# Experts' weights four rows at a time: fewer, larger loads into fewer, larger slots

## What is computed

```python
def expert_choice_moe(h, router_w, w_gate, w_up, w_down):
    affinity = jax.nn.softmax((h @ router_w).astype(F32), axis=-1)
    gate, idx = lax.top_k(jnp.swapaxes(affinity, 1, 2), cap)
    xe = jax.vmap(lambda hb, ib: hb[ib])(h, idx)
    hid = jax.nn.silu(jnp.einsum('becd,edf->becf', xe, w_gate)) * jnp.einsum('becd,edf->becf', xe, w_up)
    ye = jnp.einsum('becf,efd->becd', hid, w_down) * gate[..., None].astype(h.dtype)
```

## Time and profile before

| | |
|---|---|
| median of three runs | 3330.03 us (3327.26 to 3331.25) |
| the profiled execution | 3335.36 us |
| its span, first to last instruction | 3333.6 us |
| TensorE (PE) busy in the span | 3009.6 us, 90% |
| DMA moved | 431.71 MB in 130595 packets |
| first gate product of the experts | at 2690.03 us |
| end of the last w_down product | at 3322.50 us |

### The profile page before, as it was taken

One profiled execution on the slowest core, in us unless ns is written; L12 is line 12 of the kernel. 1 busy time (PEld: TensorE's weight loads), 2 busy tenths in 40 slices (PEclk: granted clock), 3 DMA queues, 4 the chain that ended last, 5 costly groups with the idle time before them and its releaser, 6 DMA issues. The chain is left out here.

```text
span 3333.6 us, 44206 instructions
## 1 busy us (share of the span) xinstructions
PE 3009.6 (90%) x18941; PEld 1781.4 (53%) x18941; DVE 1235.9 (37%) x2363; ACT 650.1 (20%) x1446; POOL 250.5 (8%) x347
## 2 busy tenths in 40 slices
PE   5999998999899899979999978899999789999998
PEld 2344664446675555558888863366444444444443
DVE  1052451384442499415555546544001411111111
ACT  2111341111332454112112111433100100000000
POOL 0000110000010000004324310110000000000000
PEclk8999999998879899989999989999999899999999
DMA  6441013230002311000000012300521269999998
GB/s 230 151 151 51 1 51 95 88 76 27 1 1 74 140 51 51 12 28 3 2 2 3 2 44 98 126 1 1 209 76 51 87 274 427 427 427 427 427 427 362
DMA packets 130595, 431.71 MB, mean 130 GB/s; under 512 B 28978, under 2 KB 40502, under 8 KB 102621
## 3 DMA queue, kind: packets, MB, share of 16 engines
q1 hardware_dynamic: 130402, 428.89, 33.3%
HBM read 418.21 MB, written 10.66 MB: 129 GB/s over the span
## 5 line engine op out<-in xcount | busy, mean ns | idle before, releaser
L333 PE MATMUL banks<-weight_ring,rows_turned 128*128 128x512 f32 (+1 forms) x1576 | 683.1, 594 | 52.2 <-DMA weight_ring<-in_w_in 30.5
L333 PEld LDWEIGHTS banks<-weight_ring,rows_turned 128*128 128x128 f32 x1576 | 301.2, 197 | 426.7 <-issue 406.8
L2402 PE MATMUL banks<-rows_turned,weight_ring 128*128 128x256 f32 (+1 forms) x768 | 252.8, 489 | 1.6 <-PEq L1364 1.3
L2402 PEld LDWEIGHTS banks<-rows_turned,weight_ring 128*128 128x128 f32 x768 | 147.2, 192 | 100.5 <-issue 85.7
L3615 PE MATMUL banks<-weight_ring,chosen_turned 128*64 128x512 f32 (+1 forms) x696 | 174.3, 558 | 9.5 <-DMA weight_ring<-in_w_up 6.5
L3615 PE MATMUL banks<-expert_weights_early,chosen_turned 128*64 128x512 f32 (+1 forms) x672 | 169.3, 558 | 11.2 <-DMA expert_weights_early<-in_w_up 7.6
L1432 PE MATMUL banks<-weight_ring,mix_turned 128*128 128x512 f32 x320 | 138.8, 594 | 3.8 <-ACT mix_turned L1445 2.0
L3717 DVE TENSOR_TENSOR hidden<-hidden,banks 128x512 f32<-128x512 f32 (+1 forms) x24 | 14.0, 639 | 324.2 <-PE banks L3615 324.2
L2637 PE MATMUL banks<-v_channels 64*64 64x64 f32 (+1 forms) x2880 | 122.7, 233 | 1.0 <-ACT v_channels L2757 0.3
L2637 PE MATMUL banks<-weight_ring 64*64 64x64 f32 (+1 forms) x2880 | 116.5, 227 | 0.5
L333 PE MATMUL banks<-weight_ring,branch_turned 128*128 128x512 f32 x256 | 112.8, 594 | 1.9 <-PE banks L333 1.1
(11 more groups left out here) (551 smaller groups left out, 4417.3 us busy)
## 6 DMA issues: line engine op xcount, KB each, us to landing
weight_ring<-in_w_gate SPq DMA_DIRECT2D x29, 1408.0 KB, 17.2
weight_ring<-in_w_up SPq DMA_DIRECT2D x29, 1408.0 KB, 15.1
expert_weights_early<-in_w_gate SPq DMA_DIRECT2D x28, 1408.0 KB, 19.0
expert_weights_early<-in_w_up SPq DMA_DIRECT2D x28, 1408.0 KB, 15.7
expert_weights_early<-in_w_down SPq DMA_DIRECT2D x36, 1024.0 KB, 17.3
weight_ring<-in_w_down SPq DMA_DIRECT2D x35, 1024.0 KB, 17.5
weight_ring<-in_l_w_in SPq DMA_DIRECT2D x15, 2048.0 KB, 8.6
weight_ring<-in_w_in SPq DMA_DIRECT2D x13, 2048.0 KB, 7.8
```

The costliest lines, as they stand in the source:

```text
L333: ins = kit.nc.tensor.matmul(self.bank(u), lhsT, rhs, start=(k == 0), stop=(k == nk - 1))
L2402: ins = nc.tensor.matmul(kit.ps[:, bank(u), 0:n], w[:, k, f * P:(f + 1) * P], hT[:, k, h0:h0 + n], start=(k == 0), stop=(k == KD - 1))
```

## The change

A slot holds four rows per partition, 4 x 1408 elements, 22 KB, and there are five: two early, two in the ring, one late. A chunk has 512 rows (the last of down 384: three per partition), so a partition's run is 22 KB for gate and up, 16 KB and 12 KB for down. A pair of experts has 14 chunks instead of 28. Contracted indices go in fours where they went in pairs. The tile of the weighted choice gives way to the larger late slot and lies in what the ring has left over (`spare`). The file grows by one line, so that L3615 before is L3616 after.

```diff
-    ROOM = 2 * 1408
+    ROOM = 4 * 1408
...
-        self.rooms += [flat[:, i * self.ROOM:(i + 1) * self.ROOM] for i in range(4)]
+        self.rooms += [flat[:, i * self.ROOM:(i + 1) * self.ROOM] for i in range(2)]
         self.slots = 0
+        self.spare = flat[:, 2 * self.ROOM:2 * self.ROOM + 2 * SEQ]
...
-                for k0 in range(0, KD, 2):
+                for k0 in range(0, KD, 4):
                     for e in (2 * p, 2 * p + 1):
-                        self.plan.append((2, FF, a[name][0, e][k0 * P:(k0 + 2) * P, :]))
-            for f0 in range(0, NF, 2):
-                n = min(2, NF - f0)
+                        self.plan.append((4, FF, a[name][0, e][k0 * P:(k0 + 4) * P, :]))
+            for f0 in range(0, NF, 4):
+                n = min(4, NF - f0)
...
-            at = slice(f * P, (f + 1) * P) if c < 24 else slice(f // 2 * 2 * P + f % 2, (f // 2 + 1) * 2 * P, 2)
+            at = slice(f * P, (f + 1) * P) if c < 24 else slice(f, 512, 4)
...
-                sp.dma_start(ada_b[:, 24:40].rearrange("p (i j) -> p i j", j=2), as_pairs(a["ada_b_2"][0, 3 * D:5 * D])).then_inc(c_landed.sem, 16)
+                sp.dma_start(ada_b[:, 24:40].rearrange("p (i j) -> p i j", j=4), as_fours(a["ada_b_2"][0, 3 * D:5 * D])).then_inc(c_landed.sem, 16)
...
-        early = sb("expert_weights_early", [P, 4, ExpertStream.ROOM])
+        early = sb("expert_weights_early", [P, 2, ExpertStream.ROOM])
...
-                nc.vector.tensor_scalar(normed[:, t, :].rearrange("p (i j q) -> p i q j", j=2, q=P), x[:, t, :].rearrange("p (i q j) -> p i q j", j=2, q=P),
+                nc.vector.tensor_scalar(normed[:, t, :].rearrange("p (i j q) -> p i q j", j=4, q=P), x[:, t, :].rearrange("p (i q j) -> p i q j", j=4, q=P),
...
-        weighted = sb("choice_weighted", [P, 2, TX, P])
+        weighted = weights.spare.rearrange("p (i t n) -> p i t n", i=2, t=TX)
...
-                    for k0 in range(0, KD, 2):
-                        c = W * p + 8 * mat + k0
+                    for k0 in range(0, KD, 4):
+                        c = W * p + 4 * mat + k0 // 2
...
-                        src = hid[:, f // 2 * 2 * P + f % 2:(f // 2 + 1) * 2 * P:2] if f < NF - 1 else hid[:, f * P:]
+                        src = hid[:, f0 * P + f - f0:f1 * P:f1 - f0]
...
-                for f0 in range(0, NF, 2):
-                    n = min(2, NF - f0)
-                    c = W * p + 16 + f0
+                for f0 in range(0, NF, 4):
+                    n = min(4, NF - f0)
+                    c = W * p + 8 + f0 // 2
...
-                act.wait_ge(weights.used, W * p + 8)
+                act.wait_ge(weights.used, W * p + 4)
```

More of the change, by code:

```diff
@@ L1296, in row_bc, with as_fours @@
     return v.partition_broadcast(n)
-def as_pairs(v):
-    return v.rearrange("(i p j) -> p i j", p=P, j=2)
+def as_fours(v):
+    return v.rearrange("(i p j) -> p i j", p=P, j=4)
 def as_columns(v):
@@ L2851, in second_half @@
         g2 = sb("norm2_gain", [P, KD])
-        load(kit, [(const[:, :], a["constants3"]), (g2[:, :].rearrange("p (i j) -> p i j", j=2), as_pairs(a["norm2_g_2"][0]))])
+        load(kit, [(const[:, :], a["constants3"]), (g2[:, :].rearrange("p (i j) -> p i j", j=4), as_fours(a["norm2_g_2"][0]))])
         latent_attention(kit, stream, m, a, x, s_park, h_park, y_park)
@@ L2943, in sync @@
                 sp.dma_start(normed[:, :, :], y_park).then_inc(delta_landed.sem, 16)
-                sp.dma_start(router[:, :, :].rearrange("p (i j) e -> p i j e", j=2), a["router_w_2"][0].rearrange("(i p j) e -> p i j e", p=P, j=2)).then_inc(loaded.sem, 16)
+                sp.dma_start(router[:, :, :].rearrange("p (i j) e -> p i j e", j=4), a["router_w_2"][0].rearrange("(i p j) e -> p i j e", p=P, j=4)).then_inc(loaded.sem, 16)
                 sp.dma_start(rows[:, :, :].rearrange("p i n -> p (i n)"), row_bc(rows_park[0])).then_inc(loaded.sem, 16)
@@ L3607, in gate_and_up @@
                         pe.wait_ge(added.sem, added(8 * p))
-                    for k0 in range(0, KD, 2):
-                        c = W * p + 8 * mat + k0
+                    for k0 in range(0, KD, 4):
+                        c = W * p + 4 * mat + k0 // 2
                         w = [weights.arrived(pe, c), weights.arrived(pe, c + 1)]
-                        for j in range(2):
+                        for j in range(4):
                             for i, (n0, nn) in enumerate(parts):
@@ L3616, in gate_and_up @@
                                                            w[s][:, j, n0:n0 + nn], start=(k0 + j == 0), stop=(k0 + j == KD - 1))
-                                    if j == 1 and i == 2:
+                                    if j == 3 and i == 2:
                                         ins.then_inc(weights.used, 1)
@@ L3712, in vector @@
             for p in range(pairs):
-                dve.wait_ge(weights.used, W * p + 16)
+                dve.wait_ge(weights.used, W * p + 8)
                 for i, (n0, nn) in enumerate(parts):
```

## The result

The changed kernel takes 3353.11 us (median of 4 runs, 3347.52 to 3356.32) against 3329.45 before: ratio 1.0070, 95% interval 1.0052 to 1.0087. It is slower by 20 to 24 us, outside the range of the prediction. One execution of e6 (7219 us, the profiled one) and one of the kernel before that was measured beside it (6194.56 us) were far slower than all others and stand in no ratio here.

What follows compares the result with a forecast made beforehand. The experts' stage was taken to last as long as its weight bytes take on the DMA engines at 427 GB/s. Terms -4.5 + 1.3 + 2.5 - 0.9 = -1.6 us gave 3328.4 us, range 3321.5 to 3338.

Steps and rivals of the forecast that it cites:

- Middle: Queue between expert pairs never runs dry with five slots; cost 0, margins 1.2 and 2.1 us after L, last w_down landing.
- rival (c): Slots run dry at the start of each of seven gate products, needing 5.8 us lead: 12 us lost, 3340; chance 0.13.
- Packets: Experts' weight transfers: 864 fewer packets per engine, each saving 5.2 ns that do not grow with size; -4.5 us.
- Restart: Start of the experts' stage: first issue +4.7 us later, less weight still to come -3.4; net +1.3 us.
- End: Last w_down transfers: all 24 matmuls, 5.4 us, come after the last landing instead of 2.9; +2.5 us.
- Transposes of hidden: Eleven transposes per pair reading every fourth or third element: 0 to 1.6 us a pair, inside the 2.1 margin; cost 0.
- rival (d): Strided loads of hidden much slower: eleven transposes add 3.6 us a pair, 2.1 covered, 10.5 in all: 3339; chance 0.07.
- Normalised rows: DVE's scaling with every fourth element, only the last of four exposed: 0 to +0.45 us, taken as 0.
- Small loads: Small loads ahead of the first rows and the second norm's gain, with half the packets: -0.9 us.
- (a): Packets cost nothing beyond their bytes, in the experts' transfers: +2.9 us, 3333; chance 0.2 together with (e).
- (b): Each packet's fixed part is 9.1 ns, and two longer pairs owe 1.5 us to transfer count: -5.5, or 3323; chance 0.15.
- (e): A 22 KB row of weights is cut into two packets, giving the time of (a); chance 0.2 together with (a).

Runs made afterwards that it cites:

- e6: The kernel before with a tenth room of 11 KB, the weighted choice moved into the ring's spare elements; 3325.62 us against 3330.02, ratio 0.9986.
- e1: Changed kernel with each four-row load made as two of two rows into ten 11 KB rooms, arrival and freeing still coarse; 3350.33 us, ratio 1.0059 against before.
- e5: Changed kernel with two filler matmuls ahead of each of the two waits for w_up; 3340.22 us against 3330.02 before, ratio 1.0031.
- e7: The kernel before with the ring padded to begin at a multiple of 256 bytes in each partition; 3324.23 us against 3330.02, ratio 0.9985.
- The halves: The kernels e1 to e4: changed kernel with four-row loads made as two of two rows, ten 11 KB rooms; ratios 1.0059, 1.0004, 0.9992, 0.9986 against before.
- e3: As e1, but rooms are given back two rows by two rows while TensorE still waits for all four; 3326.38 us, ratio 0.9992 against before.
- e2: As e1, but TensorE waits for the rows two by two while rooms are still freed by whole groups; 3330.00 us, ratio 1.0004 against before.
- e4: As e1, but both TensorE's waits and the freeing of rooms go two rows by two rows; 3326.08 us, ratio 0.9986 against before.
- e8: e4 with the ring at a multiple of 256 bytes; 3321.60 us against 3330.02 for the kernel before, ratio 0.9967.

## Why the prediction was wrong, step by step

**The step that failed is *Middle*, put at 0**, and it failed twice.

*The lead.* I took the 2.9 us of the first issue into an idle queue for the lead that every transfer needs. The arithmetic of the place was right: the issue was forecast at L + 29.7 and came at L + 29.73 (2752.54, then 2782.27); the queue's end was forecast at L + 33.8 and came at L + 34.4. But with one transfer left ahead of it, the load landed 12.2 us after its issue, 5.5 more than its bytes take, and the 12th load of that pair 5.2 more. Of the 13 loads at these two places that came late in the changed kernel behind the first pair, this lead is 3.8 to 5.6 us, 4.8 in the middle (3.6 at the one of the first pair); of the seven first loads of such groups that came late in e1, with half the bytes, 2.7 to 5.2, 3.7 in the middle. For the larger loads it is scattered, above 2.9 throughout, and below the 5.8 of rival (c). Part of it is their size: issued into the idle queue at the start of the stage, the first 22 KB load landed 10.58 us after its issue, 3.9 more than its bytes take, where the 11 KB load had needed 2.9. The load behind the gate's start was issued 3.6 to 4.6 us ahead of the queue's end, and lost 4.6 us over seven pairs.

*The place that I did not look at.* I followed the queue to one reuse of a slot only, the one behind the 14.65 us without weights. The 12th load reuses the slot of the last w_up rows. By the terms of the prediction: when those rows land, three loads of w_down are in the queue, 3 x 4.87 = 14.6 us, and the slot comes free after 9.67 us of matmuls, 4.9 us ahead of the end: no margin against 4.8. In e5 these loads were issued 4.7 to 4.9 us ahead and one of them lost 0.7. The 27.0 us that the sum has for the queue take the six loads of w_down as following each other without a gap, and this is the gap. And 9.67 us holds at 2.4 GHz only. The page and the chain showed that TensorE waits at w_up, and that rows two by two keep this wait at 1.8 us; that it would wait for four rows at once, twice as long, I never costed, nor what the clock does in such a wait. With the falls, the rows take 11.4 to 12.6 us, the lead is 2.0 to 3.3 and the loss 13.4 us over seven pairs.

The other terms:

- *Packets, -4.5.* The direction holds; the size can't be read closely. Held against the median of its kind (size and tile), the loads behind the first pair lost 21 us after and 3 before, and the seven pairs are 16.0 longer: so the bytes themselves took 2.0 us less, or 4.4 if the 12 KB loads, many of which come late here, are held against e5's. This term has 4.1 for them (7 x 112 packets at 5.2 ns). But the saving is not one price for each packet. A 22 KB load takes 6.67, 6.65 and 6.71 us (median; early tile, late tile, ring), where two of 11 KB took 6.68, 6.67 and 6.79: that is 2 to 3 ns for each of the 8 packets saved per engine outside the ring, and 10 in it. So most of the saving comes from the start of the ring (e7), whose price is paid once in a packet. The 3.5 ns that the prediction worked out from the Trainium skill (DMA: Bandwidth & Descriptors, "Why small descriptors are slow") lie between the two, and neither shows them. The page has 17,153 packets fewer; I had counted the weights' 14,300 and neither the completions of 112 transfers, 16 each, nor the 1,024 fewer of the small loads.
- *Restart, +1.3.* The first issue comes 9.66 us behind the first gate matmul (2699.56 and 2689.90), as forecast. The first pair's +2.4 has its own dry spot in it (its 12th load came 1.8 us late) and the longer lead of the first load; e5, without that dry spot, has +1.4.
- *End, +2.5.* Right: from the last landing (3337.90) to the last w_down matmul (3343.38) are 5.5 us, and the last landing stands 16.6 us from the span's end instead of 14.0. The halves agree: 16.8 and 16.7 with coarse arrival (e1, e3), 14.2 in both with fine (e2, e4).
- *Transposes of hidden, 0,* and with it rival (d): the eleven take 1.69 to 1.70 us, and load as before:

```profile
L3641 PEld LDWEIGHTS banks<-constants,hidden x88: 195/210/220, 2737.1 to 3323.4; 128*128 128x128 f32 x88
```

  Every fourth element costs what every second one did (210 against 209 ns). The rule of the Trainium skill (Advanced Engine Details and Errata, "SBUF Cachelines") that the prediction weighed would set the two apart; the trace does not.
- *Normalised rows, 0.* 1236 ns in place of 1188, 0.05 us for the one exposed.
- *Small loads, -0.9.* Not shown. The load of the modulation's shift landed 1.37 us behind the one ahead of it before and 0.75 after, as forecast; but in e7, where it has the same packets as before, it took 0.80. The first TensorE instruction starts 0.2 us earlier, within the 19.3 to 19.8 us of all kernels here. Among them the stage starts at points up to 12 us apart, so a term of that size ahead of it can't be read from a pair of traces.
- Two readings on the side were off. The 77.8 us of "TensorE work without waiting" hold 3.8 us of waits (TensorE is busy for 74.0 of them), so a faster transfer could give more than 3 us a pair. And the 3.6 us of rival (d) count from a contiguous load; from the 0.15 us that a transpose takes already they are 3.2.

Rivals (a), (b) and (e), all about the price of packets, and (d) are out. (c) named the right resource and side, at the lesser of two places, with a lead that was too small in the forecast and scaled with size in the rival. Its 3340 is 13 us short: it has 12 us for a place that lost 4.6, and neither the other place nor the clock. That e5 measured 3340 as well is chance.

Open: by the medians e5 is 10 us (7 to 14) over before, but its profiled execution shows 3.5 of them: the stage takes 647.0 us against 643.5, 2.5 of it *End*, 1.4 in the first pair and -0.4 in the seven pairs. Whether its other executions (3331 to 3346 us) lose more in the pairs than this one (3338.01) is not recorded, so how the loss divides between the clock and the lead alone stays open.

## What to carry to other kernels

When rooms are merged, follow the queue to every reuse of a room, at the slowest that the work ahead of it can be, and take the lead that a transfer needs from one of its own size issued behind a single other, not from one into an idle queue (up to 5.6 us here for 22 KB per partition, against 3.9 into the idle queue and 2.9 for half the size). Waiting coarsely and freeing coarsely each cost a few us once, at the end and at the start of the stage (2.5 and 4.8 here), while the other is fine; together they cost in every pair (15.0 more). So split at least one of them. A wait that doubles can take the clock with it, and a lower clock costs exactly where somebody waits for what TensorE gives back.

## What the runs showed of the hardware that I had not expected

- A load of 16 or 22 KB per partition issued with one transfer left ahead of it landed 3.6 to 5.6 us plus its bytes after the issue (14 late loads). Into an idle queue a load of 11 KB needed 2.9 us and one of 22 KB 3.9. Why the busy queue wants more is open.
- In a run of matmuls broken by waits of 1.9 us at most (before, e2, e4, e5) the granted clock stayed at 1.00. In the changed kernel all six waits of 3.6 to 3.75 us came with 3.4 or 6.8 us at 0.50, and so did four of the six between 2.03 and 2.92; in e3 five of seven between 3.7 and 3.9. e7 and e8 have one fall of 3.4 us each, behind waits of 2.8 and 2.6. These runs do not tell what sets two waits of like length apart.
- Loads of 11 KB per partition into a tile that begins 224 bytes past a multiple of 256 took 3.40 us, and 3.35 when the same tile began at a multiple. In 22 KB loads the difference from the other tiles is 0.04 to 0.06 us too, so it is paid once in a packet and not in proportion to the bytes.
